# A new order and new spacing for attention units that run beside a chain of dense matmuls

## The chip, the cores and the metric

The kernel runs on one core of one Trainium2 chip. The metric is the device time of one execution in microseconds (us). Three runs of the kernel before took 4043.72 to 4052.74 us, with a median of 4046.53 us. A profile belongs to one further execution.

## What is computed

Two transformer layers follow each other, on a sequence of 2048 tokens of width 1024, in float32. The first layer is a mixer of three kinds (spatial gating, convolution, HGRN2 recurrence), and the second is an attention layer with a gated MLP. The change touches the attention of the second layer alone:

```python
def diff_attention(q, k, v, lam, lam_init, g):
    for start in range(0, S, Q_BLOCK):                    # 128 queries, all earlier keys
        s = jnp.einsum('bqhrd,bkhrd->bhrqk', qb, kb).astype(jnp.float32) * scale
        p = jax.nn.softmax(jnp.where(mask, s, -jnp.inf), axis=-1)
        attn = p[:, :, 0] - lam * p[:, :, 1]              # two score maps per head
        outs.append(jnp.einsum('bhqk,bkhe->bqhe', attn.astype(vb.dtype), vb))
    o = rmsnorm(jnp.concatenate(outs, axis=1), g) * (1.0 - lam_init)

def stick_breaking_attention(q, k, v, g):
        z = jnp.einsum('bqhd,bkhd->bhqk', qb, kb).astype(jnp.float32) * scale
        log_1mb = jnp.where(mask, jax.nn.log_sigmoid(-z), 0.0)
        suffix = lax.cumsum(log_1mb, axis=3, reverse=True) - log_1mb
        a = jnp.where(mask, jnp.exp(jax.nn.log_sigmoid(z) + suffix), 0.0)
        outs.append(jnp.einsum('bhqk,bkhd->bqhd', a.astype(vb.dtype), vb))
```

A third mixer pools over trailing windows of 2, 4, 8 and 16 tokens. The outputs of the three go through w_out, a norm, the gate, up and down matrices of the MLP, and a last norm.

## The kernel before

**Dense work.** All large products are made as jobs of 8 (some of 6) steps. A step is three matmuls of 128x128 weights by 512 columns, high by high, high by low and low by high parts, so that float32 is kept (lines 572 to 574 in the first layer, 1509 to 1511 in the second). A job's weights come as one chunk of 512 KB by SP (`load_chunk`, issued three jobs ahead). ScalarE makes the high part (`w_high`, line 1612), VectorE the low part (`w_low`, line 1730). There are three slots of split weights and three PSUM banks for results. VectorE or ScalarE evicts a bank.

The second layer works on four groups g of 512 rows. Per group there are 8 jobs of the w_out product ("m2"), then in three chunks the gate and up jobs and the jobs of the down product ("m3"). A group has 592 steps and 12 gaps without a matmul.

**Attention.** The attention of rows of group g is cut into units u = (g, b, r, t). The head block b runs from 0 to 5: blocks 0 to 3 are differential heads with two score maps each (kind "df", 16 units per group), blocks 4 and 5 hold two stick-breaking heads each (kind "sb", 16 units). t is the tile of 128 query rows, and width(u) = (t + 1) x 128 keys. A map is made in segments of up to 512 keys, g + 1 of them. Every part of a unit is one entry in a list, and each engine walks the same list and does what is its own in it:

- ("query", u): SP loads the unit's queries in four DMAs (line 1453). ("keys", (g, b)): SP loads the keys of a head block, high and low, into the one buffer `bk_k` in two DMAs (line 1439), and waits first until all scores of the block before are made. ("values", (g, b)): SP loads the values (line 1444).
- ("scores", u, r, j): PE makes one segment of map r into one of two banks of a ring (lines 1526, 1527, and 1529 for the mask on the last segment). The first of a unit waits for its queries and keys. For df, VectorE scales it into SBUF and leaves its minimum (line 1781). For sb, ScalarE takes two sigmoids (1641, 1642).
- ("low", u): VectorE takes the minimum over the segments, of both maps at once (1789). ("exp", u, r): ScalarE takes the exponential of a whole map (1665). ("combine", u): VectorE joins the two maps to the weights (1800, 1802, 1804). ("weigh", u): for sb, VectorE scans the products of 1 - beta (1793) and multiplies (1795). Map 1 and the sb scan share one buffer, `other`, between all units.
- ("turn", u, j): PE transposes a segment of the weights (1539) and ScalarE copies it out (1674). ("product", u, j): PE multiplies by the values (1552).
- ("result", u, 0): VectorE copies the output out of PSUM (1819, 1821), ScalarE sums its squares, GpSimd takes the root. ("result", u, 1): VectorE scales. ("result", u, 2): PE transposes (1560), ScalarE copies (1687), SP waits for that copy and stores (1461).
- ("pool", g, n): SP loads the rows for pooling into the buffer that the scores use later (1472), VectorE sums windows (1831, 1835), PE multiplies (1587), ScalarE scales (1692), SP stores (1479). The first score of a group that VectorE writes waits until these stores have landed.

**The order.** `attention_order` writes the list of one group by hand. In the list of a unit u come: the queries of u + 1; all segments of map 0; ("result", u - 2, 1); ("combine", u - 1); all segments of map 1; "low" or "weigh"; where the block changes behind u, "keys" of the next block; ("result", u - 2, 2); the transposes and products of u - 1 with the two exponentials of u among them; ("result", u - 1, 0). A "pause" is an entry that does nothing: 2g of them stand before a new block, and others follow the pooling's entries.

`back_order` writes the steps of the second layer and hangs the entries of other work on them by `after[n]`. `spread` sets the list of group g + 1 at equal distances over the steps of group g, from step 2 to four jobs before its end. `whole_order` does the same for group 0 beside the last 32 jobs of the first layer. So before, each entry takes the same share of steps, whatever work it brings: 0.417, 1.170, 0.938 and 0.783 steps in groups 0 to 3, with 508, 494, 616 and 738 entries.

PE, like every engine, works its instructions in order. A matmul that waits holds all that stand behind it in the list, the dense ones too.

Of the kernel before, what the change touches and what calls it, by code (L numbers as in the profile page):

```python
# [8 lines left out]
ALU = mybir.AluOpType  # L9
ACT = mybir.ActivationFunctionType  # L10
AX = mybir.AxisListType
# [1030 lines left out]
def attention_order(units, g):  # L1042


    mine = [u for u in range(len(units)) if units[u][0] == g]
    pause = [("pause",)]
    rest = pause * (12 if g else 60)
    order = [("pool", g, 0), ("keys", units[mine[0]][:2]), ("query", mine[0])] + rest
    for n in range(len(POOL_WINDOWS)):
        order += [("pool", g, 1, n)] + rest[::3]  # L1050
    order += [("pool", g, 2)] + rest[::2]
    segs = g + 1
    for u in mine + [mine[-1] + 1, mine[-1] + 2]:
        now, old, older = u in mine, u - 1 in mine, u - 2 in mine
        diff, old_diff = now and units[u][1] < 4, old and units[u - 1][1] < 4
        new_block = now and (u == mine[0] or units[u][:2] != units[u - 1][:2])
        if new_block and u != mine[0]:
            order += pause * (2 * g)
        if u + 1 in mine:
            order.append(("query", u + 1))  # L1060
        if diff:
            order += [("scores", u, 0, j) for j in range(segs)]
        if older:
            order.append(("result", u - 2, 1))
        if old_diff:
            order.append(("combine", u - 1))
        if now:
            order += [("scores", u, 1 if diff else 0, j) for j in range(segs)]
            order.append(("low" if diff else "weigh", u))
            if u + 1 in mine and units[u + 1][:2] != units[u][:2]:  # L1070
                order.append(("keys", units[u + 1][:2]))
        if older:
            order.append(("result", u - 2, 2))
        work = []
        if old:
            work.append(("turn", u - 1, 0))
            for j in range(segs):
                if j + 1 < segs:
                    work.append(("turn", u - 1, j + 1))
                work.append(("product", u - 1, j))  # L1080
            work.append(("result", u - 1, 0))
        if diff:
            work.insert(min(2, len(work)), ("exp", u, 0))
            work.insert(min(5, len(work)), ("exp", u, 1))
        order += work
        if new_block:
            order.append(("values", units[u][:2]))
# [3 lines left out]
def back_order(jobs, units):  # L1091
# [31 lines left out]
    for g in range(NTG):  # L1123
# [9 lines left out]
        if g + 1 < NTG:  # L1133
            for t in range(4):
                spread([("last", g * 4 + t, n) for n in range(3)], at_job[base + per + 9 + 3 * t], at_job[base + per + 12 + 3 * t])
            spread(attention_order(units, g + 1), at_job[base] + 2, at_job[base + per - 4])
# [853 lines left out]
```

## Time and profile before

| | before |
|---|---|
| median of 3 runs | 4046.53 us (4043.72 to 4052.74) |
| profiled execution | 4045.1 us, span 4043.4 us |
| mean granted TensorE clock | 0.979 of 2.4 GHz |
| PE busy | 3815.1 us, 94% of the span |
| weight loads on PE busy | 3142.8 us, 78% |
| VectorE, ScalarE, GpSimd busy | 2244.4, 1640.4 and 393.4 us |
| moved by DMA | 550.72 MB, mean 136 GB/s |

The span runs from the first to the last instruction. Matmuls overlap in the array, so a matmul of 512 columns is on record for some 0.39 us although the next one starts sooner; idle time of PE is what no matmul covers. In the tables of waits each line names the instruction that stood, what let it go, the time in total, how often, and the longest. "issue" stands where the profile shows no releaser. The stretches in which attention runs beside dense work are 1362.9 to 1645.9 us (group 0), 1645.9 to 2183.0 (group 1), 2199.0 to 2835.0 (group 2) and 2852.0 to 3584.0 (group 3).

### The profile page before, as it was taken

To read this page: it belongs to the slowest core of one execution; us is meant where nothing else is said; L and a number is where in the kernel's file an instruction comes from. 1 tells how busy PE (TensorE), PEld (TensorE's weight loads), DVE (VectorE), ACT (ScalarE), POOL (GpSimd) and SP (SyncE) were. 2 spreads that over 40 slices of the span, in tenths; PEclk is the share of its full clock that TensorE was granted. 3 is DMA by queue.
4 is the path that set the end of the run, shared out by engine and by line. 5 is a ranking of instruction groups with operands and counts; after the bars stand their busy time and mean duration, and the time that the engine had idled before them with its cause. 6 is when DMAs were issued, how large, how long until landed. Compare 5 with 4: busy or idle time off the path is not lost.

```text
span 4043.4 us, 52256 instructions
## 1 busy us (share of the span) xinstructions
PE 3815.1 (94%) x19316; PEld 3142.8 (78%) x19316; DVE 2244.4 (56%) x3546; ACT 1640.4 (41%) x2994; POOL 393.4 (10%) x691
## 2 busy tenths in 40 slices
PE   7999999999999998899999899999889999999998
PEld 6888887777887766688887678888667778887886
DVE  3657675766455555555555655555555555554334
ACT  3343433344333444443443444445434354543222
POOL 1021112133221101000000000000000000000000
PEclk9999999999999999999999899999989999999999
DMA  5655554544554665634335443332634333243332
GB/s 173 199 162 168 165 169 151 176 140 151 157 165 168 194 178 156 204 95 118 117 105 151 139 130 104 111 103 75 193 109 112 97 105 91 78 140 123 96 99 79
DMA packets 347613, 550.72 MB, mean 136 GB/s; under 512 B 41696, under 2 KB 208608, under 8 KB 345824
## 3 DMA queue, kind: packets, MB, share of 16 engines
q1 hardware_dynamic: 347360, 547.37, 44.9%
q8 instruction: 156, 2.56, 0.3%
q14 instruction: 97, 0.79, 0.1%
HBM read 444.49 MB, written 102.76 MB: 135 GB/s over the span
## 4 chain that ended last, share of the span: by engine, by line
PE 61%; DVE 5%; issue 3%; ACT 3%; DMA 2%; SPq 1%; POOL 1%; ACTq 0%; POOLq 0%; DVEq 0%
PE bank L1509 12%; PE bank L1511 12%; PE bank L1510 12%; PE bk_o_ps L1552 6%; PE bank L572 3%; PE bank L574 3%; PE bank L573 3%; PE bk_turn L1539 3%; PE bk_ring L1526 2%; PE bk_ring L1527 2%; PE fr_hg_s_ps L629 1%; DVE bk_e L1781 1%; DVE bk_e L1804 1%; DVE w_lo L1730 1%; DMA bk_h<-x 1%
## 5 line engine op out<-in xcount | busy, mean ns | idle before, releaser
L1509 PE MATMUL bank<-x_hi,w_hi 128*128 128x512 f32 x2368 | 1001.8, 423 | 14.6 <-DVE w_lo L1730 6.7
L1511 PE MATMUL bank<-x_hi,w_lo 128*128 128x512 f32 x2368 | 934.7, 395 | 0.0
L1510 PE MATMUL bank<-x_lo,w_hi 128*128 128x512 f32 x2368 | 931.9, 394 | 0.0
L572 PE MATMUL bank<-x_hi,w_hi 128*128 128x512 f32 x1792 | 737.4, 411 | 15.4 <-DVE w_lo L824 10.9
L574 PE MATMUL bank<-x_hi,w_lo 128*128 128x512 f32 x1792 | 706.8, 394 | 0.0
L573 PE MATMUL bank<-x_lo,w_hi 128*128 128x512 f32 x1792 | 704.9, 393 | 0.0
L1511 PEld LDWEIGHTS bank<-x_hi,w_lo 128*128 128x128 f32 x2368 | 448.7, 189 | 100.6
L1509 PEld LDWEIGHTS bank<-x_hi,w_hi 128*128 128x128 f32 x2368 | 452.6, 191 | 93.8 <-DVE w_lo L1730 8.0
L1510 PEld LDWEIGHTS bank<-x_lo,w_hi 128*128 128x128 f32 x2368 | 452.1, 191 | 68.5 <-issue 1.3
L1612 ACT ACTIVATE w_hi<-w_in 128x1024 fp32r<-128x1024 f32 (+1 forms) x304 | 314.7, 1035 | 340.0 <-PE bank L1511 297.8
L1730 DVE TENSOR_TENSOR w_lo<-w_in,w_hi 128x1024 fp32r<-128x1024 f32 (+1 forms) x304 | 362.6, 1193 | 111.9 <-ACT w_hi L1612 111.7
L572 PEld LDWEIGHTS bank<-x_hi,w_hi 128*128 128x128 f32 x1792 | 342.4, 191 | 80.4 <-DVE w_lo L824 11.3
L574 PEld LDWEIGHTS bank<-x_hi,w_lo 128*128 128x128 f32 x1792 | 340.2, 190 | 74.0
L573 PEld LDWEIGHTS bank<-x_lo,w_hi 128*128 128x128 f32 x1792 | 342.0, 191 | 60.4 <-issue 1.2
L824 DVE TENSOR_TENSOR w_lo<-w_in,w_hi 128x1024 fp32r<-128x1024 f32 x224 | 277.3, 1238 | 128.6 <-ACT w_hi L708 128.6
L723 ACT ACTIVATE fr_res<-bank 128x512 f32<-128x512 f32 (+1 forms) x192 | 114.3, 595 | 545.5 <-PE bank L574 538.0
L1552 PEld LDWEIGHTS bk_o_ps<-bk_v,bk_wT 128*128 128x128 f32 x2176 | 291.3, 194 | 56.4 <-issue 23.9
L1552 PE MATMUL bk_o_ps<-bk_v,bk_wT 128*128 128x128 f32 (+1 forms) x2176 | 291.8, 275 | 23.6 <-ACT bk_wT L1674 23.3
L708 ACT ACTIVATE w_hi<-w_in 128x1024 fp32r<-128x1024 f32 x224 | 236.1, 1054 | 118.9 <-PE bank L574 64.4
L1781 DVE TENSOR_SCALAR_CACHE_REDUCE bk_e<-bk_ring 128x512 f32<-128x512 f32 (+3 forms) x320 | 191.0, 608 | 140.7 <-PE bk_ring L1527 95.8
L1674 ACT ACTIVATE bk_wT<-bk_turn 128x512 f32<-128x512 f32 (+2 forms) x320 | 169.1, 532 | 197.8 <-PE bk_turn L1539 195.9
L1526 PE MATMUL bk_ring<-bk_k,bk_q 128*128 128x512 f32 (+3 forms) x480 | 182.1, 379 | 57.9 <-DVE bk_e L1781 46.2
(202 smaller groups left out, 4340.6 us busy)
## 6 DMA issues: line engine op xcount, KB each, us to landing
w_in<-in_w_in SPq DMA_DIRECT2D x192, 512.0 KB, 4.3
w_in<-in_w_gate SPq DMA_DIRECT2D x88, 512.0 KB, 3.7
w_in<-in_w_up SPq DMA_DIRECT2D x88, 512.0 KB, 3.8
w_in<-in_w_down SPq DMA_DIRECT2D x64, 512.0 KB, 3.7
h1T<-fr_res SPq DMA_DIRECT2D x112, 256.0 KB, 4.1
x_in<-in_w_out SPq DMA_DIRECT2D x96, 256.0 KB, 3.2
w_in<-y1C SPq DMA_DIRECT2D x32, 512.0 KB, 4.0
bk_q<-qk_hi SPq DMA_DIRECT2D x256, 64.0 KB, 3.3
```

What stands on the lines that cost most here:

```text
L572: pe.matmul(to[:, :], w_hi[slot][:, k, :], x_hi[x % 2][:, k, :], start=k == 0, stop=False)
L573: pe.matmul(to[:, :], w_hi[slot][:, k, :], x_lo[x % 2][:, k, :], start=False, stop=False)
L574: m = pe.matmul(to[:, :], w_lo[slot][:, k, :], x_hi[x % 2][:, k, :], start=False, stop=k == KB - 1)
L708: act.activation(w_hi[j % SLOTS][:, :, :], w_in[j % 2][:, :, :], COPY).then_inc(w_hi_done, 1)
L824: dve.tensor_tensor(w_lo[j % SLOTS][:, :, :], w_in[j % 2][:, :, :], w_hi[j % SLOTS][:, :, :].bitcast(F32), ALU.subtract).then_inc(w_lo_don ...
L1509: pe.matmul(to[:, :], w_hi[slot][:, k, :], x_hi[x][:, k, :], start=k == 0, stop=False)
L1510: pe.matmul(to[:, :], w_hi[slot][:, k, :], x_lo[x][:, k, :], start=False, stop=False)
L1511: m = pe.matmul(to[:, :], w_lo[slot][:, k, :], x_hi[x][:, k, :], start=False, stop=k == parts - 1)
L1526: pe.matmul(to, queries[u % 2][:, 0, half, :], keys[:, half, ks], start=True, stop=False)
L1552: m = pe.matmul(o_ps[:, 0:P if b < 4 else HD], wT[product_at[u, j] % 2][:, i, :], value, start=s == 0, stop=s == t)
L1612: act.activation(w_hi[(BEFORE + j) % SLOTS][:, 0:parts, :], w_in[j % 2][:, 0:parts, :], ACT.Copy).then_inc(w_hi_done, 1)
L1730: dve.tensor_tensor(w_lo[slot][:, 0:parts, :], w_in[j % 2][:, 0:parts, :], w_hi[slot][:, 0:parts, :].bitcast(F32), ALU.subtract).then_inc( ...
```

## The change

Three things change. First, `attention_order` gives each entry a room, and `back_order` and `whole_order` place an entry by the sum of the rooms before it, over the same steps as before. Second, the order within a unit is new. The first two segments of map 0 come first, then ("combine", u - 1) and ("result", u - 2, 1). After that the remaining segments alternate with transposes and products of u - 1, with the first minimum and the first exponential among them. Then come ("result", u - 2, 2), ("result", u - 1, 0), the second minimum and the second exponential, or "weigh". "values" and "keys" stand at the end. Keys and queries of a group's first block come before the pooling. Third, there is one minimum per score map (`lowest`), and each exponential waits for its own.

```diff
 def attention_order(units, g):
...
     mine = [u for u in range(len(units)) if units[u][0] == g]
-    pause = [("pause",)]
-    rest = pause * (12 if g else 60)
-    order = [("pool", g, 0), ("keys", units[mine[0]][:2]), ("query", mine[0])] + rest
+    segs = g + 1
+    order = []
+
+    def put(room, *unit):
+        order.append((room, unit))
+
+    put(0, "keys", units[mine[0]][:2])
+    put(0, "query", mine[0])
+    put(60, "pool", g, 0)
     for n in range(len(POOL_WINDOWS)):
-        order += [("pool", g, 1, n)] + rest[::3]
-    order += [("pool", g, 2)] + rest[::2]
-    segs = g + 1
+        put(12, "pool", g, 1, n)
+    put(8, "pool", g, 2)
     for u in mine + [mine[-1] + 1, mine[-1] + 2]:
...
+        size = (units[u][3] + 1) / 4 if now else 0
+        old_size = (units[u - 1][3] + 1) / 4 if old else 0
         if new_block and u != mine[0]:
-            order += pause * (2 * g)
+            put(4 + 2 * g, "pause")
         if u + 1 in mine:
-            order.append(("query", u + 1))
-        if diff:
-            order += [("scores", u, 0, j) for j in range(segs)]
-        if older:
-            order.append(("result", u - 2, 1))
-        if old_diff:
-            order.append(("combine", u - 1))
-        if now:
-            order += [("scores", u, 1 if diff else 0, j) for j in range(segs)]
-            order.append(("low" if diff else "weigh", u))
-            if u + 1 in mine and units[u + 1][:2] != units[u][:2]:
-                order.append(("keys", units[u + 1][:2]))
-        if older:
-            order.append(("result", u - 2, 2))
-        work = []
+            put(0, "query", u + 1)
+        if old_diff and not diff:
+            put(1 + 2.5 * old_size, "combine", u - 1)
+        scores = [("scores", u, r, j) for r in range(2 if diff else 1) for j in range(segs)] if now else []
+        turns = []
         if old:
-            work.append(("turn", u - 1, 0))
+            turns.append(("turn", u - 1, 0))
             for j in range(segs):
                 if j + 1 < segs:
-                    work.append(("turn", u - 1, j + 1))
-                work.append(("product", u - 1, j))
-            work.append(("result", u - 1, 0))
+                    turns.append(("turn", u - 1, j + 1))
+                turns.append(("product", u - 1, j))
+        room = {"scores": 1.5 if diff else 3, "turn": 1.2, "product": 2}
         if diff:
-            work.insert(min(2, len(work)), ("exp", u, 0))
-            work.insert(min(5, len(work)), ("exp", u, 1))
-        order += work
+            for unit in scores[:min(2, segs)]:
+                put(room["scores"], *unit)
+            scores = scores[min(2, segs):]
+            if old_diff:
+                put(1 + 2.5 * old_size, "combine", u - 1)
+        if older:
+            put(0.5, "result", u - 2, 1)
+        rows = 0
+        while scores or turns:
+            if scores:
+                unit = scores.pop(0)
+                put(room["scores"], *unit)
+            if diff and (not scores or scores[0][2] == 1) and rows == 0:
+                put(0.3, "low", u, 0)
+                rows = 1
+            if len(turns) > len(scores) or turns and len(scores) < 2 * len(turns):
+                put(room[turns[0][0]], *turns.pop(0))
+            if rows == 1 and (not scores or len(scores) < segs):
+                put(1 + 2 * size, "exp", u, 0)
+                rows = 2
+        if older:
+            put(0.8, "result", u - 2, 2)
+        if old:
+            put(0.8, "result", u - 1, 0)
+        if diff:
+            put(0.3, "low", u, 1)
+            put(1 + 2 * size, "exp", u, 1)
+        elif now:
+            put(1 + 6 * size, "weigh", u)
         if new_block:
-            order.append(("values", units[u][:2]))
+            put(0, "values", units[u][:2])
+        if u + 1 in mine and units[u + 1][:2] != units[u][:2]:
+            put(0, "keys", units[u + 1][:2])
     return order
...
-            spread(attention_order(units, g + 1), at_job[base] + 2, at_job[base + per - 4])
+            work = attention_order(units, g + 1)
+            total, done, start, stop = sum(room for room, _ in work), 0, at_job[base] + 2, at_job[base + per - 4]
+            for room, unit in work:
+                after[int(start + (stop - start) * done / total)].append(unit)
+                done += room
...
-                    act.wait_ge(low_ready, df_to[u] + 1)
+                    act.wait_ge(low_ready, 2 * df_to[u] + r + 1)
...
+            def lowest(u, r):
+                for j in range(units[u][0] + 1):
+                    _, at, uses = seg_at[u, r, j]
+                    dve.wait_ge(ring_read[at], uses + 1)
+                dve.tensor_reduce(low[:, u % 2, r:r + 1], top[:, u % 2, r * 4:r * 4 + units[u][0] + 1], AX.X, ALU.min).then_inc(low_ready, 1)
+
```

In `whole_order` the list of group 0 is placed in the same way. In `weigh` the reduction for df is gone, and VectorE's `unit` calls `lowest` for "low" and `weigh` for "weigh" alone.

## Rows read from the trace of the kernel before

**Rows 1.** The page, part 1: engine, busy us, share of the span, instructions.

```profile
PE 3815.1 (94%) x19316; PEld 3142.8 (78%) x19316; DVE 2244.4 (56%) x3546; ACT 1640.4 (41%) x2994; POOL 393.4 (10%) x691
```

**Rows 2.** Busy time by stretch: length, PE, PEld, DVE, ACT, POOL; clock, DMA.

```profile
1362.90:1645.90 283.00, 252.31 (x1233) 194.87 (x1232) 141.60 (x340) 121.22 (x301) 26.64 (x67) 0.97 0.62 176
1645.90:2183.00 537.10, 521.58 (x2643) 429.31 (x2642) 292.79 (x525) 232.19 (x461) 29.53 (x72) 0.98 0.41 121
2199.00:2835.00 636.00, 601.73 (x3148) 495.18 (x3146) 355.62 (x600) 283.10 (x530) 33.71 (x80) 0.97 0.40 116
2852.00:3584.00 732.00, 672.17 (x3630) 553.01 (x3628) 411.47 (x665) 329.93 (x594) 36.56 (x80) 0.97 0.38 107
3658.90:3925.30 266.40, 266.36 (x1184) 220.81 (x1185) 108.66 (x122) 70.43 (x87) 3.50 (x8) 0.99 0.34 107
```

**Rows 3.** Waits of PE, whole span: waiter <- releaser: us, times, longest.

```profile
PE bk_ring L1526 <- DVE bk_e L1781: 46.2, 33, 3.4
PE bk_o_ps L1552 <- ACT bk_wT L1674: 23.3, 24, 4.0
PE bk_turn L1587 <- issue: 21.5, 3, 14.4
```

**Rows 4.** Waits of PE, 1363 to 1646 us, beside group 0's attention.

```profile
PE bk_o_ps L1552 <- ACT bk_wT L1674: 16.7, 21, 2.3
PE bk_ring L1526 <- issue: 6.5, 5, 2.2
```

**Rows 5.** Groups of instructions by shape, DVE: busy us, mean ns | idle before.

```profile
L1802 DVE TENSOR_SCALAR bk_ratio<-bk_inverse,bk_total,bk_lam 128x1 f32<-128x1 f32 x64 | 17.5, 273 | 2.4
...
L1804 DVE SCALAR_TENSOR_TENSOR bk_e<-bk_e,bk_ratio 128x1792 f32<-128x1792 f32 x4 | 8.3, 2085 | 0.1
...
L1793 DVE TENSOR_TENSOR_SCAN bk_e<-bk_e,bk_zero 128x1920 f32<-128x1920 f32 x4 | 16.6, 4158 | 0.0
...
L1795 DVE TENSOR_TENSOR bk_e<-bk_e 128x1920 f32<-128x1920 f32 x4 | 8.6, 2157 | 0.1
```

**Rows 6.** Timeline 2973.0 to 2992.6, one change of head block: start us, us.

```profile
2973.90 0.40 PE L1527 MATMUL bk_ring<-bk_k,bk_q 128*128 128x512 f32 x1
...
2974.40 0.58 SPq L1439 DMA_DIRECT2D bk_k<-qk_hi  x1
...
2975.03 0.61 SPq L1439 DMA_DIRECT2D bk_k<-qk_lo  x1
...
2976.34 0.27 PE L1560 MATMUL bk_turn<-ident,bk_o 128*128 128x128 f32 x1
...
2977.04 0.33 SPq L1461 DMA_DIRECT2D m2C<-bk_y  x1
...
2991.77 0.39 PE L1526 MATMUL bk_ring<-bk_k,bk_q 128*128 128x512 f32 x1
...
2992.23 0.40 PE L1526 MATMUL bk_ring<-bk_k,bk_q 128*128 128x512 f32 x1
...
2992.52 0.69 DVE L1781 TENSOR_SCALAR_CACHE_REDUCE bk_e<-bk_ring 128x512 f32<-128x512 f32 x1 [1.62 <-PE bk_ring L1527]
```

**Rows 7.** DMA issues of the keys' second half, groups 0 to 3; us to landing.

```profile
bk_k<-qk_lo SPq DMA_DIRECT2D x6, 256.0 KB, 5.2
...
bk_k<-qk_lo SPq DMA_DIRECT2D x6, 512.0 KB, 7.2
...
bk_k<-qk_lo SPq DMA_DIRECT2D x6, 768.0 KB, 9.5
...
bk_k<-qk_lo SPq DMA_DIRECT2D x6, 1024.0 KB, 12.0
```

**Rows 8.** Busy time by stretch, as rows 2: a wait of PE, and behind it.

```profile
2220.90:2225.20 4.30, 0.00 (x0) 0.00 (x0) 4.27 (x6) 1.37 (x2) 0.00 (x0) 1.00 0.61 164
2225.20:2228.60 3.40, 3.40 (x8) 2.72 (x9) 3.33 (x5) 1.69 (x2) 0.00 (x0) 0.51 1.00 327
```

More of the change, by code:

```diff
@@ L1163, in whole_order @@
         beside[start + n // 2][n % 2 * 4].append(("prepare", n))
-    spread(attention_order(units, 0), KB * start + 12, KB * (J1 - 4))
+    work = attention_order(units, 0)
+    total, done = sum(room for room, _ in work), 0
+    for room, unit in work:
+        at = int(KB * start + 12 + (KB * (J1 - start - 4) - 12) * done / total)
+        beside[at // KB][at % KB].append(unit)
+        done += room
     beside[J1 - 10][0].append(("xl", 0))
@@ L1782, in scores @@
                                   accum_out=top[:, u % 2, r * 4 + j:r * 4 + j + 1]).then_inc(ring_read[at], 1)
+            def lowest(u, r):
[3 more added lines that the diff above has]
+                dve.tensor_reduce(low[:, u % 2, r:r + 1], top[:, u % 2, r * 4:r * 4 + units[u][0] + 1], AX.X, ALU.min).then_inc(low_ready, 1)
             def weigh(u):
-                segs, w = units[u][0] + 1, width(u)
+                w = width(u)
                 for n, at, uses in [seg_at[key] for key in seg_at if key[0] == u][-2:]:
                     dve.wait_ge(ring_read[at], uses + 1)
-                if kind_of(u) == "df":
-                    dve.tensor_reduce(low[:, u % 2, :], top[:, u % 2, :].rearrange("p (r j) -> p r j", j=4)[:, :, 0:segs], AX.X, ALU.min).then_inc(low_ready, 1)
-                    return
                 me.done(dve.memset(other(u)[:, w:w + 1], 1.0))
@@ L1882, in unit @@
                     scores(*of)
-                elif kind in ("low", "weigh"):
+                elif kind == "low":
+                    lowest(*of)
+                elif kind == "weigh":
                     weigh(*of)
```

## The prediction, made before the changed kernel ran

> **What bounds the kernel now.** I read the page's busy time first: TensorE (PE) is busy 94% of the span, VectorE 56% [rows 1], so the time is PE's work plus the time in which PE stands. Then the stretches, by the busy table [rows 2]. The difference of length and PE busy time is PE's idle time: 283.0 - 252.3 = 30.7 us beside the attention of group 0, then 15.5, 34.3 and 59.8 us beside groups 1 to 3, 140 us in all; the last row, 384 dense steps with no attention, has none, and gives the price of a step, 266.4 / 384 = 0.694 us. So the change works on four stretches in which PE loses 140 us, plus what the clock loses after a wait.
>
> What PE waits for there is in the table of waits [rows 3]: 46.2 us for a bank of the score ring that VectorE has not read yet (33 waits), 23.3 us for ScalarE's copy of transposed weights, 21.5 us before the pooling product. In group 0 alone [rows 4], 16.7 of the 23.3 us lie, and 6.5 us in five waits of a score for nothing that the table can name: a group has five changes of head block, and those five waits stand at them, where the new keys come in.
>
> **The change, part by part.** A "room" is now a share of the stretch. Adding up the put calls gives 600, 1009, 1417 and 1825 rooms for groups 0 to 3, over 212, 578, 578 and 578 steps: one room is 0.353, 0.573, 0.408, 0.317 steps.
>
> *Scores between transposes and products: -36 us.* Before, all scores of a unit follow each other, and the combine (in group 3 about 2.1 us, with 0.27 us for the ratio [rows 5]) sits between the two maps; VectorE then reads late and PE meets a full ring. Now two scores come, the combine with room 1 + 2.5 size, and then one transpose or product after each score. A score's two matmuls start 0.46 us before the next score's, its eviction takes 0.69 us on VectorE [rows 6]; with an equal piece of other work between, the ring keeps up. I take off 36 of the 46.2 us; bounds 46 and 0 (VectorE just as late).
>
> *Products further from their transposes in group 0: -12 us.* In the first four blocks the exponential's room now lies between (1.1 instead of 0.4 steps); the two stick-breaking blocks keep 0.4 steps. Of 23.3 us I take off half; bounds 23 and 0.
>
> *Pooling: -6 us.* Its product comes at room 108, step 34 in group 3, where it was unit 35 of 0.78 steps, step 27. Of the 21.5 us waits, 7 steps (4.9 us) in group 3 and all in groups 1 and 2 go, some 12 us. But between this product and the first score there are 8 rooms, 2.5 steps, instead of 6 units, 4.7 steps, and VectorE may not write the first scores before the pooled rows are stored: I give back 6. On SP the pool's load now goes behind two key and four query loads; 60 rooms (19 steps) cover that. Bounds -21 and +8.
>
> *A minimum per map: 0.* 64 more small reductions on VectorE, with idle time beside them; bound +10, if each is met by PE.
>
> *Longer VectorE work right before its reader: +16 us.* The first transpose of a unit now follows its combine by 1.5 + (1 + 2.5 size) + 0.5 + 1.5 rooms, counted from the second score. At size 3.5 in group 3 that is 13.25 rooms, 4.2 steps, 2.9 us, with two scores 3.8 us. VectorE needs 0.75 us until it reads that score (2991.77 to 2992.52), 0.69 and 0.08 for reading it [rows 6], then about 0.5 and 2.1 us for the combine [rows 5]: 4.1 us, and 108.7 / 384 = 0.28 us of dense work per step [rows 2]. PE waits some 0.6 us, 10 us over 16 units; 3 in group 2, where a room is longer. Stick-breaking: the scan and multiply take 4.2 + 2.2 us [rows 5] against 23.5 rooms, 7.4 steps, 5.2 us of cover; with the score and the rooms after it that is even, 3 us. Bounds 0 and +50. Queued behind the scan on VectorE are evictions and low parts of chunks, which have some 13 steps of slack.
>
> *Keys later: +106 us.* This is the term that decides. Before, the keys of the next block are put directly after the last score's minimum. In the trace [rows 6] the last score starts at 2973.90, SP issues the two loads at 2974.40 and 2975.03, and the next block's first score comes at 2991.77, 17.4 us later. The second load lands 5.2, 7.2, 9.5 and 12.0 us after its issue [rows 7], so the pair takes 5.8, 7.8, 10.1, 12.6 us from the first issue: hidden in groups 1 to 3, and the cause of the 6.5 us in group 0, where little stands between. Now "keys" is the last put of a unit: behind ("result", u-2, 2), ("result", u-1, 0), the second minimum and the room of the second exponential. Only the pause, 4 + 2g rooms, and a query with no room stand before the next score.
>
> SP runs ahead of PE until something holds it. What holds it now is the store of ("result", u-2, 2), which waits until that transpose is copied out: PE starts the transpose at 2976.34, SP the store at 2977.04 [rows 6]; with the store's own 0.33 us, keys go 1.0 us after. From that transpose to the next block's first score there are 0.8 + 0.8 + 0.3 + (1 + 2(g+1)) + (4 + 2g) rooms: 8.9, 12.9, 16.9, 20.9, which are 3.1, 7.4, 6.9, 6.6 steps or 2.2, 5.1, 4.8, 4.6 us, plus 0.25 us of transpose. PE therefore waits 5.8 + 1.0 - 2.2 - 0.25 = 4.35 us in group 0 (1.3 us of it is there today), then 3.45, 6.05 and 8.75 us. PE works in order, so its dense matmuls stand too, and nothing covers this. Four such changes per group: 4 x (3.05 + 3.45 + 6.05 + 8.75) = 85 us. The fifth change follows a stick-breaking unit: the store lies further back, and SP is held by the chunk loads, which wait for a low part made two jobs before its use; if SP is five steps ahead (an estimate from that distance) PE waits 1.9, 4.3, 6.9 us, with SP at PE's step 5.4, 7.8, 10.4. Halfway, with 2.2 in group 0: 21 us. Bounds of the whole term: 136 us, if SP is never ahead, and 20 us, if the pairs travel at 327 GB/s, the highest rate among my rows [rows 8]. I take the landing rows, since they are these same transfers.
>
> *Clock: +10 us.* After PE had stood for 4.3 us the granted clock was 0.51 (1.2 GHz) in the next 3.4 us [rows 8], 1.7 us lost. Fifteen new waits of 3 us and more: 25 us; ring and pool waits that go give back 15 (estimate). Bounds -15 and +40.
>
> *Values and queries*: values move behind the exponential's or scan's room, as do their first readers; 0, bound +5. Queries keep a unit of lead.
>
> Sum: -36 - 12 - 6 + 0 + 16 + 106 + 10 = +78 us. The profiled execution took 4045.1 us (span 4043.4), 1.4 us under the median of the runs, so **4123 us**.
>
> **Rivals.** *Keys arrive in time.* The place is the first score of a block; if the pairs come at 327 GB/s, the key term is 20 us and the clock's 6 lower: 4045 + 78 - 106 + 20 - 6 = 4031 us; with no wait at all 4007. It turns faster once the key waits sum to under some 30 us, 1.5 us per change. For it: while PE stands, chunk loads stop and leave the transfer engines to the keys. Against: the 1 MB load took 12.0 us, and group 0 shows the wait today. Chance 0.14.
> The Trainium skill's page "DMA: Bandwidth & Descriptors" (section "Anatomy of one DMA — SWDGE (gpsimd) path") fits a DMA's time as 2.0 us plus bytes over 436 GB/s, for the other issuing path. By that rule a 2.1 MB pair would take 6.8 us, the key term would be near 27 us, and the kernel would come out at about 4044 us, unchanged; the landing rows disagree (12.0 us), and I give it 0.03.
>
> *No change*: key waits of 25 to 45 us, paid for by the ring; 4038 to 4054 us, chance 0.08 with the rule above.
>
> *Combine and scan become the wait.* If in groups 2 and 3 each of 64 units waits 0.6 us more at its first transpose, because the second exponential (issued 12 rooms before the combine) or a low part of a chunk comes first: +40, 4163 us. Chance 0.15.
>
> *The alternation does nothing*: the ring waits stay because VectorE's lateness comes from dense work; +36, 4159 us. Chance 0.05.
>
> My forecast keeps 0.58. About 0.2% (8 us) is what a measurement of this kernel can tell from no change. Faster 0.14, within 0.08, slower 0.78. The range goes from 4040, which leaves out the keys in time, to 4190: the key term's upper bound adds 30, the combine's 40. My forecast's own range is 4075 to 4175 us.
>
> **What would show it.** Right: waits of the line-1526 matmul put down to nothing or to the key loads, twenty of them, growing to 8 us in group 3, with both key loads issued within a few microseconds of the score; waits for VectorE's score reads down to some 10 us; a clock near 0.5 behind each long wait. Wrong: key loads issued 10 us and more before the score, or landing in 7 us; then the alternation shows alone and the kernel is faster. Waits of the line-1539 transposes for VectorE of over 40 us would be the third case.

## The result and the profile after

The changed kernel takes 4160.58 us (median of 4 runs, 4157.02 to 4168.29), where the kernel before takes 4049.64 us (4 runs beside them). The ratio is 1.0277, with a 95% interval of 1.0255 to 1.0299: 111 us slower by the medians. The forecast was 4123 us with a range of 4040 to 4190 us: right in direction and mechanism, and some 38 us too low.

In what follows a line of the back half has a number higher by 35 than before: the first score matmul was 1526 and is 1561, the transposes of the weights 1539 and 1574, the products 1552 and 1587, the key loads 1439 and 1474. VectorE's combine (1804 before) is 1842, and the multiply behind the stick-breaking scan (1795 before) is 1833.

Part 1 of the page after, TensorE's row first. The span is 4159.0 us:

```profile
PE 3832.2 (92%) x19316; PEld 3169.1 (76%) x19316; DVE 2240.4 (54%) x3610; ACT 1632.7 (39%) x2994; POOL 528.0 (13%) x691
```

Against [rows 1] PE's busy time grew by 17.1 us with the same 19316 instructions, and the span by 115.6 us. So 98.5 us of the growth is time in which PE stands, and 17.1 us is slower work. VectorE has 64 more instructions, the second minima, and less busy time. No engine became the bound.

Busy time by stretch, after (the attention of groups 0 to 3; columns as in rows 2):

```profile
1363.40:1683.50 320.10, 264.77 (x1233) 205.55 (x1232) 140.59 (x356) 119.47 (x301) 29.65 (x68) 0.92 0.56 155
1683.50:2251.40 567.90, 530.80 (x2642) 436.00 (x2640) 290.63 (x541) 230.37 (x459) 45.74 (x72) 0.96 0.40 114
2267.80:2920.40 652.60, 600.38 (x3149) 498.09 (x3148) 354.75 (x617) 280.19 (x530) 78.99 (x80) 0.96 0.40 113
2936.80:3696.80 760.00, 670.97 (x3630) 560.37 (x3629) 411.18 (x681) 328.46 (x594) 106.85 (x80) 0.95 0.37 104
```

Length less PE busy is 55.3, 37.1, 52.2 and 89.0 us, where [rows 2] gave 30.7, 15.5, 34.3 and 59.8 us. The sum went from 140 to 234 us, so 93 of the 98.5 us of new standing lie in the four stretches. The clock column fell from 0.97 or 0.98 to between 0.92 and 0.96.

The waits of PE over the whole span, after (what stood <- what let it go: us, times, longest; DMA as what let go is a load that landed):

```profile
PE bk_ring L1561 <- issue: 122.3, 20, 13.6
...
PE bk_turn L1574 <- DVE bk_e L1842: 18.4, 12, 5.2
PE bk_o_ps L1587 <- DMA bk_v<-vC: 11.3, 5, 3.9
...
PE bk_o_ps L1587 <- ACT bk_wT L1709: 10.0, 13, 2.1
PE bk_turn L1574 <- DVE bk_h L1951: 9.7, 4, 4.1
...
PE bk_turn L1622 <- issue: 9.3, 3, 8.8
...
PE bk_ring L1561 <- DVE bk_e L1816: 7.6, 3, 5.4
...
PE bk_ring L1561 <- DMA bk_q<-qk_lo: 5.7, 5, 1.8
```

The first row is the result: twenty waits of a first score, five per group, 122.3 us. Of the waits of [rows 3], the ring's went from 46.2 to 7.6 us, that for ScalarE's copies from 23.3 to 10.0, the pooling product's from 21.5 to 9.3. New or grown are waits of the transposes for VectorE (rows 1574; 7.5 us in all before), for values (none before) and for queries (1.0 us before).

One change of head block in group 3, on the timeline after (start us, us); it answers to [rows 6]:

```profile
3169.79 0.40 PE L1562 MATMUL bk_ring<-bk_k,bk_q 128*128 128x512 f32 x1
...
3173.44 0.27 PE L1595 MATMUL bk_turn<-ident,bk_o 128*128 128x128 f32 x1
...
3174.14 0.32 SPq L1496 DMA_DIRECT2D m2C<-bk_y  x1
...
3174.51 0.59 SPq L1474 DMA_DIRECT2D bk_k<-qk_hi  x1
...
3175.14 0.61 SPq L1474 DMA_DIRECT2D bk_k<-qk_lo  x1
...
3187.35 0.77 PE L1561 MATMUL bk_ring<-bk_k,bk_q 128*128 128x512 f32 x1 [8.86 <-issue]
```

Read it from below. The first score started after a wait of 8.86 us, 12.84 us after the first key load was issued at 3174.51. That load went out 1.07 us after the result's transpose, directly behind the store, and 4.7 us after the unit's last score. Before, the distance from the last score to the issue was 0.50 us [rows 6].

Landing times of the keys after: both halves for group 3, then the second half for groups 2 to 0 (KB each, median us from issue to landing):

```profile
bk_k<-qk_hi SPq DMA_DIRECT2D x6, 1024.0 KB, 7.7
bk_k<-qk_lo SPq DMA_DIRECT2D x6, 1024.0 KB, 12.0
...
bk_k<-qk_lo SPq DMA_DIRECT2D x6, 768.0 KB, 10.2
...
bk_k<-qk_lo SPq DMA_DIRECT2D x6, 512.0 KB, 8.5
...
bk_k<-qk_lo SPq DMA_DIRECT2D x6, 256.0 KB, 5.0
```

The second halves are those of [rows 7], at most 1.3 us longer: the loads take as long with PE standing as beside running work.

The same block change by stretch (columns as in rows 2): the wait, and three stretches behind it.

```profile
3178.50:3187.30 8.80, 0.00 (x0) 0.00 (x0) 0.00 (x0) 0.00 (x0) 0.00 (x0) 0.68 0.99 212
...
3187.35:3190.80 3.45, 3.45 (x8) 2.80 (x9) 2.07 (x6) 0.04 (x1) 0.00 (x0) 0.50 0.76 267
3190.80:3194.20 3.40, 3.40 (x14) 2.70 (x14) 3.33 (x4) 0.59 (x1) 0.00 (x0) 0.83 0.00 0
3194.20:3197.60 3.40, 3.40 (x23) 2.92 (x22) 2.80 (x9) 1.73 (x4) 0.00 (x0) 1.00 0.51 152
```

In the wait all five engines stand. The granted clock falls while PE stands, is at 0.50 (1.2 GHz) for 3.45 us after that, and is back at full speed only in the last row. The instruction counts show what this costs: 8 matmuls in 3.45 us, and 23 in 3.40 us (their sizes differ). The three rows behind the wait lose an estimated 3.45 x 0.50 + 3.40 x 0.17 = 2.3 us.

### The profile page after: what moved, and what is told of

Its sections match the earlier page's. It is cut to its first block, busy times and chain, and to the rows that moved or that the text cites. A ratio compares the mean times of both kernels' runs of the same rounds, so it can differ in the third digit from the quotient of the medians.

```text
span 4159.0 us, 52384 instructions
## 1 busy us (share of the span) xinstructions
PE 3832.2 (92%) x19316; PEld 3169.1 (76%) x19316; DVE 2240.4 (54%) x3610; ACT 1632.7 (39%) x2994; POOL 528.0 (13%) x691
## 4 chain that ended last, share of the span: by engine, by line
PE 61%; issue 5%; DVE 4%; DMA 3%; ACT 2%; SPq 1%; POOL 1%; ACTq 0%; POOLq 0%; DVEq 0%
PE bank L1544 12%; PE bank L1546 12%; PE bank L1545 12%; PE bk_o_ps L1587 6%; PE bank L572 3%; PE bank L574 3%; PE bk_turn L1574 3%; PE bank L573 3%; PE bk_ring L1561 2%; PE bk_ring L1562 2%; DMA x_in<-in_w_out 1%; PE fr_hg_s_ps L629 1%; SPq L1488 1%; DVE bk_e L1842 1%; DMA w_in<-m2C 0%
## 5 line engine op out<-in xcount | busy, mean ns | idle before, releaser
L572 PEld LDWEIGHTS bank<-x_hi,w_hi 128*128 128x128 f32 x1792 | 344.0, 192 | 82.3 <-DVE w_lo L824 11.3
L1378 POOL TENSOR_SCALAR bk_ss<-bk_ss 128x1 f32<-128x1 f32 x128 | 99.8, 779 | 1715.7 <-ACT bk_y L1716 1715.7
L1561 PE MATMUL bk_ring<-bk_k,bk_q 128*128 128x512 f32 (+3 forms) x480 | 192.6, 401 | 135.5 <-issue 122.3
L1587 PE MATMUL bk_o_ps<-bk_v,bk_wT 128*128 128x128 f32 (+1 forms) x2176 | 288.0, 274 | 21.5 <-DMA bk_v<-vC 11.3
```

Source lines behind the costliest of these rows:

```text
L572: pe.matmul(to[:, :], w_hi[slot][:, k, :], x_hi[x % 2][:, k, :], start=k == 0, stop=False)
L1561: pe.matmul(to, queries[u % 2][:, 0, half, :], keys[:, half, ks], start=True, stop=False)
L1587: m = pe.matmul(o_ps[:, 0:P if b < 4 else HD], wT[product_at[u, j] % 2][:, i, :], value, start=s == 0, stop=s == t)
```

## The experiments

All ratios are to the kernel before, run on the same chip in the same session, with a 95% interval. The kernel before had medians of 4047 to 4052 us in these sessions (e1 to e4, e5 to e8, e9 to e12), so a difference between experiments of different sessions holds to some 5 us.

**e1: the keys right behind the last score.** The changed kernel with one entry moved.

```diff
                 unit = scores.pop(0)
                 put(room["scores"], *unit)
+                if not scores and u + 1 in mine and units[u + 1][:2] != units[u][:2]:
+                    put(0, "keys", units[u + 1][:2])
...
-        if u + 1 in mine and units[u + 1][:2] != units[u][:2]:
-            put(0, "keys", units[u + 1][:2])
```

> The changed kernel with one thing put back: the keys of the next block stand directly behind the last score of the unit, not at the unit's end. Theory (the late keys cost the time): the twenty waits of 122 us fall to the five of group 0 (some 7 us) and the clock gives back some 25 us, so about 4025 us, faster than the kernel before. Rival (the combines and scans right before their readers, or the new spacing itself, cost the time): the waits move to the transposes behind, and it stays above 4100 us.

Measured: 4033.46 us, ratio 0.9954 (0.994 to 0.9968). Waits of PE in e1:

```profile
PE bk_ring L1561 <- issue: 24.1, 10, 5.3
PE bk_turn L1574 <- DVE bk_e L1842: 21.5, 14, 5.2
...
PE bk_o_ps L1587 <- DMA bk_v<-vC: 12.4, 5, 4.6
```

The key waits fall by 98 us and the time by 127 us. The place of one list entry that brings no work to PE is worth more than the whole difference between the two kernels. Of the 24.1 us that stay, all but 1.1 lie in groups 2 and 3, where even keys issued 0.50 us after the last score land up to 5.3 us late; the expectation had put them in group 0, and the time is 8 us above its 4025. In group 3 of e1 the first three changes have 8 to 9 us from a last score to the next block's first score, without the wait. In [rows 6] it was 17.9 us, because there the transposes and products came behind the last score.

**e2: the other way round.** The kernel before, with "keys" moved to the end of the unit's list.

```diff
                 order.append(("low" if diff else "weigh", u))
-            if u + 1 in mine and units[u + 1][:2] != units[u][:2]:
-                order.append(("keys", units[u + 1][:2]))
...
             order.append(("values", units[u][:2]))
+        if u + 1 in mine and units[u + 1][:2] != units[u][:2]:
+            order.append(("keys", units[u + 1][:2]))
     return order
```

> The kernel before with that one thing done alone: the keys are put at the end of the unit's list, everything else untouched. Theory: PE waits for keys at all twenty changes of block, 2 to 6 us each, since here the pauses and SP's lead cover some 5 to 7 us; some 75 us more, about 4120 us. Rival (the keys matter only in the new order): no key wait over 2 us and 4047 us.

Measured: 4096.51 us, ratio 1.011 (1.0095 to 1.0124).

```profile
PE bk_ring L1526 <- DVE bk_e L1781: 47.7, 33, 3.9
PE bk_ring L1526 <- issue: 34.9, 13, 6.2
```

The sign was as expected; the size, 45 us, was not. In the old order all transposes and products of the unit before stand between the result's store and the next block's first score. In groups 2 and 3 the first score came 12 to 16 us after the keys' issue, as long as the pair needs, and 8 of the 10 waits there are under 2 us; 18.4 of the 34.9 us lie in group 0. So the late place alone is not what costs 127 us. It does so because the new order has also moved that cover: the alternation puts transposes and products ahead of the last score, and ("result", u - 2, 2) with its store now stands behind all of them. e4 below shows the first of the two by a run. The second is read from the lists, and no run moved the store alone.

**e3: values earlier too.** e1 with "values" put in front of ("result", u - 2, 2) instead of at the end.

```diff
+        if new_block:
+            put(0, "values", units[u][:2])
         if older:
             put(0.8, "result", u - 2, 2)
...
-        if new_block:
-            put(0, "values", units[u][:2])
```

> e1 and also the values put right behind the last product of the block before, ahead of the second exponential or the scan. Theory: the waits for values (11 us in the changed kernel) go, 8 to 12 us less than e1, about 4015 us. Rival (those waits are covered once the keys are, or move to the next wait of the same unit): within 4 us of e1.

Measured: 4028.07 us, ratio 0.9939 (0.9927 to 0.9952), which overlaps e1's interval. The waits for values (12.4 us in e1) are gone from the list, and in group 0 waits for queries (3.7 us in e1) take their place:

```profile
PE bk_ring L1561 <- DMA bk_q<-qk_lo: 11.7, 9, 2.7
```

What one load gains there, the next one gives back for the most part. The gain of 5 us lies between the theory's 8 to 12 and the rival's 4.

**e4: no alternation.** e1, but transposes and products come only when all scores of the unit are out.

```diff
-            if len(turns) > len(scores) or turns and len(scores) < 2 * len(turns):
+            if turns and not scores:
```

> e1 without the alternation: transposes and products begin when the last score is out; rooms, combine's place and keys as in e1. Theory (alternation thins the ring waits): waits of scores for VectorE's reads come back to 40 us and more and the time is 35 to 45 us above e1. Rival (the alternation does nothing; it is the combine's place between the second and third score that helps): ring waits under 15 us and a time within 10 us of e1.

Measured: 4037.67 us, ratio 0.9963 (0.9949 to 0.9978), against e1's 0.9954: the intervals overlap. The ring waits are the theory's, the time is the rival's. The waits of PE in e4:

```profile
PE bk_ring L1561 <- DVE bk_e L1816: 47.5, 22, 5.4
...
PE bk_o_ps L1587 <- ACT bk_wT L1709: 17.1, 30, 2.1
```

Without alternation the ring waits are back at 47.5 us (e1: 9.4), so it is the alternation that removes them. But the wait for the combine, 21.5 us in e1, is gone from e4's list, and key waits are 2.8 instead of 24.1 us. As the change spaces it, the alternation exchanges one wait for two others, of 43 us together.

**e5: PE kept busy in the key waits.** The changed kernel. In front of each new block's first score PE makes small matmuls into the bank that the score will overwrite. `FILL` is a table with a count for each block change, 43 to 226.

```diff
...
+                if r == 0 and j == 0 and units[u - 1][:2] != (g, b):
+                    pe.wait_ge(ring_read[at], uses)
+                    for _ in range(FILL[g][b]):
+                        pe.matmul(ring[at][:, 0:P], bf_ident[:, :], bf_mask[1][:, :], start=True, stop=True)
```

> The changed kernel, but in front of the first score of each new block TensorE runs small matmuls (128 columns, result thrown away) for about as long as the wait that the changed kernel's trace shows there, 0.4 us less each, 114 us in all. The keys still come when they come, so the waits' length stays; only TensorE's being idle in them goes. Theory (the clock behind the key waits costs by itself): idle time falls from 304 to some 195 us, time at half clock falls from 281 to 150-180 us, and the kernel gains half of that, 50 us at most: some 4115 us, between 4105 and 4135. Rival (the clock is low for other reasons, the waits are the whole cost): 4155 to 4165 us. Second rival (the small matmuls don't hold the clock, or run longer than the waits): slower, 4165 to 4190.

Measured: 4123.7 us, ratio 1.0189 (1.0174 to 1.0205). In e5 the small matmuls are line 1561, and the score is line 1568. First the group of PE's instructions (busy us, mean ns; they overlap, so that 1959 of them cover only 113.0 us), then the page's row, then the wait that is left:

```profile
L1561 PE MATMUL bk_ring<-bk_bf_mask,bk_bf_ident 128*128 128x128 bf16 x1959 | 113.0, 219 | 0.6 <-issue 0.6
```

```profile
PE 3910.0 (95%) x21275; PEld 3251.0 (79%) x21275; DVE 2239.4 (54%) x3610; ACT 1633.1 (40%) x2994; POOL 528.7 (13%) x691
```

```profile
PE bk_ring L1568 <- issue: 15.9, 14, 2.5
```

The keys come no sooner: small matmuls and remaining waits make 113.0 + 15.9 = 128.9 us in place of 122.3. PE's own work, 3910.0 - 113.0 = 3797.0 us, is 35 us shorter than the changed kernel's 3832.2, and the time is 37 us shorter. The mean granted clock is 0.983 instead of 0.966. The theory's range held, although its idle times did not: span less PE's busy time was 326.8 us in the changed kernel, not 304, and is 211.6 us in e5. So of the 127 us that e1 won, about 36 are the clock behind the waits, and some 90 the waits themselves.

**e6: three rooms made equal.** The order of e1, with room 1 for the combine, the exponentials and the scan.

```diff
-            put(1 + 2.5 * old_size, "combine", u - 1)
+            put(1, "combine", u - 1)
...
-                put(1 + 2 * size, "exp", u, 0)
+                put(1, "exp", u, 0)
...
-            put(1 + 6 * size, "weigh", u)
+            put(1, "weigh", u)
```

> Keys early as in e1, same order, but the rooms of the combine, of the exponentials and of the scan with its multiply are 1 instead of growing with their size: what the second phrase of the change does, taken away alone. Theory (room by work hides VectorE's and ScalarE's long pieces): waits of the weight transposes for VectorE rise from some 30 to 60-100 us, ScalarE's copies from 12 to about 22; 4060 to 4100 us. Rival (the order alone does it, the spacing nothing): 4028 to 4040 us. The key waits should grow a little in either case, since the exponentials' rooms lay behind the keys.

Measured: 4150.89 us, ratio 1.0256 (1.0242 to 1.0269).

```profile
PE bk_turn L1574 <- DVE bk_e L1833: 60.9, 28, 5.4
PE bk_turn L1574 <- DVE bk_e L1842: 42.9, 34, 7.6
```

These rooms by work are worth 117 us in the new order. Without them the transposes meet VectorE's scan with its multiply (60.9 us; 3.3 in e1) and its combine (42.9 us; 21.5 in e1), and the mean granted clock is 0.969 (e1: 0.982). Those 103.8 us are just above what the first theory said, and the time is far above it. Of the growth against e1, 75 us are time in which PE stands and 50 us are longer PE busy time (3851.2 us for 3800.8), which the expectation left out. Two parts of the expectation were wrong: the waits for ScalarE's copies fell to 7.9 us instead of rising, and the key waits stayed at 24.0.

**e7: a minimum per map alone.** The kernel before, with `low` split as in the change: each exponential waits for its own map's minimum.

```diff
             order += [("scores", u, 0, j) for j in range(segs)]
+            order.append(("low", u, 0))
...
-            order.append(("low" if diff else "weigh", u))
+            order.append(("low", u, 1) if diff else ("weigh", u))
```

> The kernel before with a minimum per score map alone: 64 more small reductions on VectorE, each first exponential waits for its own map only. Theory (prediction's term of 0, bound +10): within 8 us of before. Rival: the first exponential starts a map earlier and ScalarE's and the ring's waits shrink, 5 to 20 us faster. Second rival: the reduction stands in front of an eviction that TensorE waits for, 64 x 0.3 us, up to 20 us slower.

Measured: 4058.93 us, ratio 1.0028 (1.0016 to 1.0039): 6 to 16 us slower, as the second rival had it.

```profile
PE bk_ring L1527 <- DVE bk_e L1782: 52.8, 30, 5.3
PE bk_turn L1588 <- issue: 24.6, 3, 15.2
...
PE bk_o_ps L1553 <- ACT bk_wT L1675: 17.0, 21, 1.8
```

The copies' wait falls by 6.3 us against [rows 3], the ring's grows by 6.6, the pooling product's by 3.1. Alone, this part costs a little and gains nothing. Whether it does so by standing in front of an eviction, as that rival says, the waits do not show. What it costs or brings in the new order was not tried.

**e8: two edits aimed at what e3 still waits for.** e3, in which the last unit of a block keeps its scores together, so that the keys go earlier, and the combine has more room.

```diff
+        last = u + 1 in mine and units[u + 1][:2] != units[u][:2]
...
-            if len(turns) > len(scores) or turns and len(scores) < 2 * len(turns):
+            if turns and not (last and scores) and (len(turns) > len(scores) or len(scores) < 2 * len(turns)):
...
-            put(1 + 2.5 * old_size, "combine", u - 1)
+            put(2 + 4 * old_size, "combine", u - 1)
```

> e3 with two edits aimed at its two largest waits in the attention: the last unit of a block keeps its scores together, so that the keys can go earlier (key waits 23.5 us), and the combine's room grows from 1 + 2.5 to 2 + 4 times its size (waits for the combine 21.3 us). Theory: key waits fall to 3-6 us, combine waits to 5-10 us, ring waits grow by 5-10 us; with a little clock, 4005 us, between 3998 and 4015. Rival (the waits move on: VectorE or the ring takes what the two give): 4020 to 4030 us.

Measured: 3986.6 us, ratio 0.9847 (0.9832 to 0.9862), 1.5% faster than the kernel before and 4.2% faster than the changed one. That is 11 us below the range of the theory. Waits of PE in group 3's stretch of e8 (2800 to 3580 us, its lines one higher):

```profile
PE bk_ring L1562 <- DVE bk_e L1817: 11.5, 6, 5.0
...
PE bk_ring L1562 <- issue: 1.9, 3, 0.9
...
PE bk_turn L1575 <- DVE bk_e L1843: 0.7, 1, 0.7
```

In e3 the same stretch had 18.4 us of key waits and 16.5 us for the combine:

```profile
PE bk_ring L1561 <- issue: 18.4, 4, 5.5
PE bk_turn L1574 <- DVE bk_e L1842: 16.5, 8, 5.2
```

Now it is 1.9 and 0.7.

**e9 and e10: each of the two edits alone**, on e3.

> e3 with the first of e8's two edits alone: the last unit of a block keeps its scores together and its keys go right behind them; the combine's room as in the change. Theory (the two edits work on separate waits): key waits fall from 23.5 to under 8 us, combine waits stay near 21 or grow a little, about 4010 us (4003 to 4018). Rival (only together do they gain, since the time between the last score and the next block's first score is what the combine's room stretches): 4022 to 4030 us.

> e3 with the second of e8's edits alone: 2 + 4 instead of 1 + 2.5 times its size for the combine's room. Theory: combine waits fall from 21 to below 8 us, key waits stay near 20 us, about 4005 us (3998 to 4015). Rival: the room is paid for by all other rooms getting smaller, so that waits for the exponentials and the keys take what the combine gives, 4022 to 4030 us.

Measured: e9 4002.88 us, ratio 0.9879 (0.9864 to 0.9894); e10 4012.19 us, ratio 0.9902 (0.9882 to 0.9922). In e9 the key waits fall to 2.0 us and the combine's stays:

```profile
PE bk_turn L1575 <- DVE bk_e L1843: 22.0, 14, 5.2
```

In e10 it is the reverse:

```profile
PE bk_ring L1561 <- issue: 23.8, 9, 5.7
...
PE bk_turn L1574 <- DVE bk_e L1842: 8.5, 4, 5.1
```

The gains against e3 are 25 and 16 us, together 41, as large as e8's gain (4028.07 - 3986.6 = 41.5 us; by the ratios 24, 15 and 37 us). So the two waits are independent as far as these runs tell. A part does move: the ring's waits are 14.8 us in e9, where e3 had 9.9. For e9 the lower edge of the expected time was met; e10 came out at the upper part of its range.

**e11: e8 without any alternation** (the edit of e4 on e8).

> e8 without any alternation: in every unit all scores come first, as in e4, then transposes and products; rooms, keys and values as in e8. Theory (with the combine's room mended, alternation is worth what it takes off the ring, some 30 us of waits): 4010 to 4025 us, ring waits 40-50 us. Rival (as e4 against e1: alternation is worth next to nothing once other waits take its place): 3985 to 3995 us.

Measured: 4021.79 us, ratio 0.9934 (0.9915 to 0.9952).

```profile
PE bk_ring L1561 <- DVE bk_e L1816: 40.8, 26, 6.5
```

The trace is of an execution of 4033.35 us, 12 us above the median. With the keys in time and the combine covered, the alternation is worth 35 us. It was worth nothing measurable in e4 against e1, because there its gain went into the combine and the keys.

**e12: the pooling later.** e8 with more room around the pool's load (90 for 60 in groups 2 and 3) and behind its product (16 for 8).

> e8 with more room between the pool's load and its sums in groups 2 and 3 (90 for 60) and behind the pool's product (16 for 8). Theory: the 11.7 us of waits at the pooling product (2 of them) go and a wait of the first scores behind it shrinks, 6 to 15 us faster than e8: 3972 to 3982 us. Rival (the wait's cause, pool rows that VectorE finishes late, moves with it, or the units squeezed together wait as much more): 3984 to 3992 us.

Measured: 3988.61 us, ratio 0.9844 (0.983 to 0.9859), the same as e8. The pooling product's waits fall from 11.7 to 7.2 us, and the ring's grow from 15.6 to 20.3. The rival held.

## Why the prediction was right, and where not

The waits named as the mark of the forecast came as said: the first score's matmul (line 1526, now 1561), twenty times, put down to nothing, 8.6 to 9.2 us in the first three changes of group 3. The keys were issued 1.07 us after the result's transpose in twelve of the twenty, and later in the others, mostly behind a weight chunk (1.0 was said). The clock sign held: in the 3.4 us behind each of the twenty waits the granted clock is 0.50 to 0.61. One sign was badly put. "Key loads issued 10 us and more before the score" was to mean wrong, but a score that waits for its keys starts when they have landed, and in groups 2 and 3 the loads were issued 10.2 to 13.5 us before it. What the working meant is the distance to the point at which PE began to stand: 4.0 us in the rows above (3174.51 to 3178.5). By its terms:

- *Keys (+106).* Measured are 122.3 us of waits, of which 6.5 stood there before [rows 4]: +115.8. By group the five waits sum to 21.4, 22.7, 31.3 and 46.9 us. A single wait of the first three changes was about 4.4, 5.3, 7.1 and 8.9 us, against 4.35, 3.45, 6.05 and 8.75 in the working. Two details failed and partly cancel. The fourth change was shorter (6.64 us in group 3), since the combine of the last df unit stands in front of the first stick-breaking score with a room of its own, which the sum left out. The fifth was longer in group 3, 13.56 us, where the working took the middle between 6.9 us (SP five steps ahead) and 10.4 us (SP at PE's step). On the timeline (start us, us):

```profile
3521.34 0.47 SPq L1498 DMA_DIRECT2D m2C<-bk_y  x1
...
3527.50 1.22 DVE L1765 TENSOR_TENSOR w_lo<-w_in,w_hi 128x1024 fp32r<-128x1024 f32 x1
...
3529.13 0.58 SPq L1474 DMA_DIRECT2D bk_k<-qk_hi  x1
```

After the store SP waited 6.9 us with a weight chunk for VectorE, whose scan (4.42 us, from 3520.84) and multiply (2.29 us) came before the low part of 3527.50. The keys went out behind that chunk, 8.5 us after the result's transpose. The working had chunk loads that wait for a low part; that the scan can hold that low part was not in it.

- *Clock (+10).* e5 shows some 36 us behind the key waits, where the working had 25. Its price held, 1.7 us for a wait [rows 8]: behind the twenty waits the first 3.4 us lose 1.6 us each on average (an estimate from the clock of those stretches). Its count did not: it took fifteen of the twenty waits, and nothing behind the first 3.4 us, where the rows shown above lose 0.6 us more. Since PE's busy time grew by 17.1 us, some 19 us came back elsewhere, where the working had 15. So the term measured +17.
- *Ring (-36), copies (-12), pooling (-6).* The waits fell by 38.6, 13.3 and 12.2 us. As waits the first two were right or a little low, and the pooling gave twice what was said. As time the ring's -36 is there only when nothing else takes it up: e4 against e1 shows nothing, e11 against e8 shows 35 us.
- *Longer VectorE work before its reader (+16).* Waits of the weights' transposes for VectorE went from 7.5 us in the trace before to 35.0 us (18.4 and 9.7 in the rows above, 3.6 and 3.3 in smaller ones): +27.5, inside the bounds of 0 to 50. In group 3 the combine alone makes 16.5 us, where the working had 10. The third rival is this mechanism; it is in the trace, below the 40 us at which it would have decided. e6 shows that the rooms are what held it down.
- *Values and queries (0, bound +5).* This failed: 11.3 us of waits for values and 5.7 for queries (1.0 before). The working said that the first readers move with the loads, and did not price group 0, where all five waits for values and all five for queries lie.
- *A minimum per map (0, bound +10).* Alone it costs 6 to 16 us (e7).

The wait terms add up to 115.8 - 38.6 - 13.3 - 12.2 + 27.5 + 11.3 + 4.7 = +95 us, against 98.5 us more time in which PE stands. With +17 us of PE's busy time they explain 112 of the 115.6 us by which the span grew. The sum said +78, 38 us less. No single term carries that: values and queries are 16 us above the working, VectorE's work 11.5, the keys 10 and the clock 7, while ring, copies and pooling took off 10 us more than said. So the mechanism was right, and that the total missed by no more is in part luck, since these errors go both ways. Where the 19 us in PE's busy time came from was not tried; in e8, with the waits for keys and combine gone for the most part, it is 3793.1 us, 22 us under the kernel before.

The rivals: *keys arrive in time* fell, since the landing times did not change. From the first issue to the first score the trace has 12.84 us in group 3. By the Trainium skill, "DMA: Bandwidth & Descriptors" (section "Anatomy of one DMA — SWDGE (gpsimd) path"), 2.0 us plus bytes over 436 GB/s, the pair of 2.1 MB, counted as one transfer, would take an estimated 6.8 us; that is stated for the other issuing path, and the trace of these loads does not agree: the second half alone landed 12.1 us after its issue. e1 is what the kernel would have been with the keys nearly in time: 4033 us, where this rival said 4031. *No change* fell with 122.3 us of key waits, where it had 25 to 45. *The alternation does nothing* fell with the ring waits of 7.6 us.

## What to carry to other kernels

An entry that costs its own engine nothing still needs a price: the time from its issue to its landing, counted forward to its first reader. Its issue is counted from what stands before it in SP's queue, above all a store or a load that waits for another engine. Whoever fills gaps by alternating work should look at what that work was covering before; here it covered the loads of the next block. And a gain in one wait shows in the time only when the next waits in line are mended too, so judge a part again after the others are in order: the alternation was worth nothing at first and 35 us in the end.

## What the runs showed of the hardware

- The key pair moves slowly even when no engine works. In those 8.8 us the transfer engines were busy 0.99 of the time and moved 212 GB/s. The halves landed one behind the other, 4.9 us apart, 7.8 and 12.1 us after their issues at 3174.51 and 3175.14. In another stretch of full share, [rows 8], it was 327 GB/s. So a full busy share is not one fixed rate. Each key half goes into 64 of the 128 partitions and a weight chunk into all 128; no run changed that, so whether it sets the rate stays open.
- What SP issued behind the pair came late with it. A weight chunk of 512 KB issued at 3175.79 landed after 12.5 us (the median of its line is 3.9 us), about 1 us behind the keys, and the four query loads behind it after 11.9 to 13.1 us (medians 3.3 and 2.9).
- Small matmuls whose result nobody reads brought the mean granted clock from 0.966 back to 0.983 (e5), the changed kernel's 122.3 us of key waits being filled with 113.0 us of them. It is a way to price the clock behind a wait apart from the wait. As a remedy it gives under a third of what an earlier load gives (37 of 127 us).
- GpSimd's busy time rose from 393.4 to 528.0 us with the same 691 instructions, and to 527 to 534 us in the others of the new order at rooms by work. The trace shows where: in the 128 pairs of one-column instructions of the result's root (lines 1378 and 1380), whose means went from 271 to 779 ns and from 571 to 1078 ns. With VectorE idle they take 0.19 and 0.55 us, as before, and so do the eight that ran beside its evictions (line 1816). Beside VectorE's scan the first of a pair takes 1.63 us in the mean (46 times) and up to 4.14, and beside its multiply the second takes 1.93 us (47 times). No pair ran beside the scan or the multiply in the kernel before; the new order puts them there. Why they take longer beside these and not beside evictions, no run varied. Spans on GpSimd are rough, and no wait of PE is put down to it.
